# A decoder kernel whose statistics are summed by TensorE: two fp32r matmuls over a split operand for one plain fp32 matmul

## What is computed

```python
for l in range(DEPTH):                       # 2
    h = h + 0.5 * swiglu(rms(h, norm_ffn1), ffn1_wi, ffn1_wo)
    z = rms(h, norm_mix) @ w_in              # conv, spatial gate, q, k/v, gates
    y_a = conv_module(z_conv) @ conv_out     # depthwise conv of 31, LayerNorm over 512
    y_b = spatial_gating(z_sgu) @ sgu_out    # rms over 512
    y_c = nsa(q, k, v) @ nsa_out             # rms of every q and k head over 64
    h = h + (g_a * y_a + g_b * y_b + g_c * y_c) @ w_out
    h = h + cross_attention(rms(h, norm_xattn), rms(mem))   # k heads normed over 128
    h = h + 0.5 * swiglu(rms(h, norm_ffn2), ffn2_wi, ffn2_wo)
```

## Time and profile before

| | before |
|---|---|
| time, median of 3 runs | 2720.15 us (2715.23 to 2720.67) |
| span of the profiled execution | 2716.9 us |
| TensorE busy | 2664.1 us |
| VectorE busy | 1326.2 us |
| ScalarE busy | 1100.5 us |
| GpSimd busy | 1230.2 us |

### The profile page before, as it was taken

The page is one execution under the profiler, slowest core; times in us unless marked ns, Lnnn a source line. Parts: engine busy times, 40 slices in busy tenths (PEclk is TensorE's granted clock), DMA queues, the critical chain, the costliest instruction groups (busy, mean ns, idle before and its releaser), DMA issues.

```text
span 2716.9 us, 36975 instructions
## 1 busy us (share of the span) xinstructions
PE 2664.1 (98%) x13132; PEld 2137.3 (79%) x13132; DVE 1326.2 (49%) x1834; ACT 1100.5 (41%) x1664; POOL 1230.2 (45%) x616
## 2 busy tenths in 40 slices
PE   8999999989999999999999999999899999999999
PEld 6888888766678868888888888887667788788887
DVE  5221258786535554252541212777865364543533
ACT  5322242446644454222342223434476445542222
POOL 4444456672235424444444434567522354344443
PEclk9999999999999999999999999999999999999999
DMA  4334433222224313333333353432122342233332
GB/s 133 95 99 113 115 98 87 70 55 55 55 78 117 109 47 107 94 99 95 91 95 101 93 132 92 111 79 68 49 55 63 86 124 85 62 101 101 93 100 78
DMA packets 493612, 243.41 MB, mean 90 GB/s; under 512 B 49468, under 2 KB 491174, under 8 KB 493478
## 3 DMA queue, kind: packets, MB, share of 16 engines
q1 hardware_dynamic: 492960, 241.49, 32.0%
q10 hardware_dynamic: 518, 0.13, 0.0%
HBM read 239.46 MB, written 2.10 MB: 89 GB/s over the span
## 4 chain that ended last, share of the span: by engine, by line
PE 65%; issue 16%; POOL 8%; DVE 5%; ACT 3%; POOLq 2%; DVEq 1%; ACTq 0%; DMA 0%; SPq 0%
PE pg L636 20%; PE pg L639 19%; PE pg L642 19%; POOL wL L585 7%; PE pA L706 2%; DVE convb L1740 1%; PE pA L911 1%; PE pA L858 1%; POOLq L612 1%; POOLq L614 1%; DVE prob L1902 0%; POOL wsn L610 0%; ACT prob L1156 0%; ACT wH L1156 0%; ACT hH L1156 0%
## 5 line engine op out<-in xcount | busy, mean ns | idle before, releaser
L585 POOL TENSOR_TENSOR wL<-raw,wH 128x1024 fp32r<-128x1024 f32 (+1 forms) x472 | 1084.9, 2300 | 1453.2 <-ACT wH L1156 1449.4
L636 PE MATMUL pg<-gxH,wH 128*128 128x512 f32 (+1 forms) x2448 | 960.6, 392 | 3.6 <-DVE gxL L1601 3.1
L642 PE MATMUL pg<-gxH,wL 128*128 128x512 f32 (+1 forms) x2448 | 948.7, 388 | 0.0
L639 PE MATMUL pg<-gxL,wH 128*128 128x512 f32 (+1 forms) x2448 | 944.1, 386 | 0.0
L1156 ACT ACTIVATE wH<-raw 128x1024 fp32r<-128x1024 f32 (+1 forms) x472 | 475.8, 1009 | 834.3 <-PE pg L642 673.5
L636 PEld LDWEIGHTS pg<-gxH,wH 128*128 128x128 f32 x2448 | 461.0, 188 | 110.7 <-issue 18.4
L639 PEld LDWEIGHTS pg<-gxL,wH 128*128 128x128 f32 x2448 | 461.2, 188 | 93.6 <-issue 7.1
L642 PEld LDWEIGHTS pg<-gxH,wL 128*128 128x128 f32 x2448 | 461.0, 188 | 93.2 <-issue 3.9
L642 PE MATMUL pg<-hH,wL 128*128 128x512 f32 x992 | 392.7, 396 | 0.0
L636 PE MATMUL pg<-hH,wH 128*128 128x512 f32 x992 | 390.5, 394 | 1.5 <-DVE hL L1657 1.5
L639 PE MATMUL pg<-hL,wH 128*128 128x512 f32 x992 | 390.6, 394 | 0.0
(11 more groups left out here) (234 smaller groups left out, 2208.8 us busy)
## 6 DMA issues: line engine op xcount, KB each, us to landing
raw<-in_ffn_wi SPq DMA_DIRECT2D x352, 256.0 KB, 3.1
raw<-in_w_in SPq DMA_DIRECT2D x200, 256.0 KB, 3.3
raw<-in_ffn_wo SPq DMA_DIRECT2D x128, 256.0 KB, 3.0
raw<-in_ffn_wo SPq DMA_DIRECT2D x64, 192.0 KB, 2.6
raw<-in_xkv SPq DMA_DIRECT2D x32, 256.0 KB, 3.0
raw<-in_w_out SPq DMA_DIRECT2D x32, 256.0 KB, 3.0
raw<-in_sgu_out SPq DMA_DIRECT2D x32, 128.0 KB, 2.2
raw<-in_conv_out SPq DMA_DIRECT2D x32, 128.0 KB, 2.2
```

Source lines behind the costliest of these rows:

```text
L585: pool.tensor_tensor(wL[:, s % 4, 0:n, :], raw[:, s % 2, 0:n, :], wH[:, s % 4, 0:n, :].bitcast(F32), ALU.subtract)\
L636: mm(o, wH[:, s, k, :], rh(k), start=(k == 0), stop=False)
L639: mm(o, wH[:, s, k, :], rl(k), start=False, stop=False)
L642: last = mm(o, wL[:, s, k, :], rh(k), start=False, stop=(k == kt - 1))
```

## The change

Two fp32r tiles are added, `sacH` and `sacL`. Once `sacc` is complete, `stat_given` copies it to `sacH` (rounded to fp32r) and subtracts that from `sacc` into `sacL`, on VectorE, ahead of the semaphore. TensorE multiplies both, one after the other into the same bank. The ones matrices become fp32r tiles with fp32 views for the places that stay as they were, which are the 31-column statistic and the one-column matmuls.

```diff
         sacc = sb("sacc", [P, T])
+        sacH = sb("sacH", [P, T], F32R)
+        sacL = sb("sacL", [P, T], F32R)
...
-        ones = sb("ones", [P, P])
-        bdon = sb("bdon", [P, P])
+        onesR = sb("onesR", [P, P], F32R)
+        bdonR = sb("bdonR", [P, P], F32R)
+        ones, bdon = onesR[:, :].bitcast(F32), bdonR[:, :].bitcast(F32)
...
             def stat(l, s, weights, n=T):
 
                 pe.wait_ge(stat_in, risen(stat_in, l, s + 1 if s < 6 else s))
-                mm(pO[:, 0:n], weights[:, :], sacc[:, 0:n], start=True, stop=True)\
+                if n < T:
+                    mm(pO[:, 0:n], bdon[:, :], sacc[:, 0:n], start=True, stop=True)\
+                        .then_inc(stat_mm, 1)
+                    return
+                mm(pO[:, :], weights[:, :], sacH[:, :], start=True, stop=False)
+                mm(pO[:, :], weights[:, :], sacL[:, :], start=False, stop=True)\
                     .then_inc(stat_mm, 1)
...
                 def middle(key, s):
                     bank = t_bank(key)
                     pe.wait_ge(stat_in, risen(stat_in, l, s))
-                    weights = bdon if key in ("q2", "q3") else ones
-                    mm(bank[:, :], weights[:, :], sacc[:, :], start=True, stop=True)\
+                    weights = bdonR if key in ("q2", "q3") else onesR
+                    mm(bank[:, :], weights[:, :], sacH[:, :], start=True, stop=False)
+                    mm(bank[:, :], weights[:, :], sacL[:, :], start=False, stop=True)\
                         .then_inc(st_mm, 1)
...
             def stat_given(s):
 
+                dve.drain()
+                dve.tensor_copy(sacH[:, :], sacc[:, :])
+                dve.drain()
+                TTt(sacL[:, :], sacc[:, :], sacH[:, :].bitcast(F32), ALU.subtract)
                 dve.drain().then_inc(stat_in, 1)
...
                 def squares(src, n=T):
                     dve.drain()
                     TTt(sacc[:, 0:n], src, src, ALU.mult)
-                    stat_given(None)
+                    if n < T:
+                        dve.drain().then_inc(stat_in, 1)
+                    else:
+                        stat_given(None)
```

More of the change, by code:

```diff
@@ L678, in ffn @@
                                  before=norm_ready(l, n_norm) if c == 0 else None,
-                                 between=within(14, lambda: stat(l, s_norm, ones))
+                                 between=within(14, lambda: stat(l, s_norm, onesR))
                                  if c == 1 and s_norm else None)
                             if c == 1 and s_norm == 0:
-                                stat(l, s_norm, ones)
+                                stat(l, s_norm, onesR)
                         first = 1
@@ L738, in _ @@
                 unit(l, U_CONV + 1, 0, KD, gH, gL)
-                unit(l, U_CONV + 2, 0, KD, gH, gL, between=within(6, lambda: stat(l, 1, ones)))
+                unit(l, U_CONV + 2, 0, KD, gH, gL, between=within(6, lambda: stat(l, 1, onesR)))
                 for g in range(GROUPS):
@@ L747, in _ @@
                     unit(l, U_KV + j, 0, KD, gH, gL)
-                unit(l, U_KV + 4, 0, KD, gH, gL, between=within(6, lambda: stat(l, 2, bdon)))
+                unit(l, U_KV + 4, 0, KD, gH, gL, between=within(6, lambda: stat(l, 2, bdonR)))
                 v_rows(0)
                 unit(l, U_KV + 5, 0, KD, gH, gL)
-                stat(l, 3, bdon)
+                stat(l, 3, bdonR)
                 def cmp_ready(k):
@@ L795, in _ @@
                     if j == 2:
-                        stat(l, 5, bdon)
+                        stat(l, 5, bdonR)
                     if 3 <= j < 7:
@@ L802, in _ @@
                          lambda k: gxL[:, 4 * i + k, :])
-                stat(l, 7, bdon)
+                stat(l, 7, bdonR)
                 def gates_turned():
@@ L1017, in _ @@
                     if h == 4:
-                        stat(l, 12, ones)
+                        stat(l, 12, onesR)
                     if h == 6:
@@ L1027, in _ @@
                     if m == 0:
-                        stat(l, 13, ones)
+                        stat(l, 13, onesR)
                         xv_turned(1)
```

## The result

| | before | after |
|---|---|---|
| time, median | 2718.74 us (4 runs) | 2750.15 us (2748.06 to 2754.58, 4 runs) |
| ratio after / before | | 1.0116, 95% interval 1.0104 to 1.0128 |
| span of the profiled execution | 2716.9 us | 2746.3 us |
| TensorE busy | 2664.1 us | 2662.4 us |
| VectorE busy | 1326.2 us | 1378.4 us |

A forecast was written before the change was run, and what follows sets the result against it. TensorE, busy 98% of the span, was taken as the bound. Stalls of 16.75 us a layer, 33.5 for two, plus 0.5 in the prologue, less 10.9 saved, gave +23.1 us: 2743 us, range 2719 to 2757.

The forecast's parts named there:

- The bound and the sign: Whole kernel: TensorE, busy 98%, bounds it; stalls of 34.0 us less 10.9 saved make it 23.1 us slower.
- The saving per statistic: TensorE, 26 plain fp32 statistics become two fp32r matmuls: 0.42 us saved for each, 10.9 in all.
- The split, undisturbed: VectorE in stat_given: copy, subtraction and two drains raise the semaphore 1.28 us later when GpSimd doesn't interfere.
- The collisions by the timeline of before: Added copy and subtraction meet GpSimd's operations where they stand: 2.65 us at first key statistic, 2.6 at second, per layer.
- the FFN norm: Norm ahead of the second FFN: TensorE already waits, subtraction comes behind a wL; 3.4 us a layer, quiet 1.28.
- the norm before cross-attention: Added work unused there; a wL over the copy delays the query copy 3.4 us, TensorE 1.8; 1.2 taken a layer.
- s=7: Second query pair's statistic: a 2.40 us wL begins just ahead of the subtraction; stall 3.7 us, 3.0 taken a layer.
- Third query pair: Its squares: the split delays four convolution steps and the maxima TensorE waits for; 2.6 us a layer, quiet 1.28.
- the soaking rival: Attention stretch: existing TensorE waits and freer convolution steps absorb the added stalls; 7.1 us faster, 2713 us; chance 0.08.
- all others: Remaining statistics (mean, query pairs, memory keys, norms ending an FFN): slack of 2 us or more; 0.7 us a layer.
- The variance: Variance of the conv branch, GpSimd idle: 0.6 us a layer, up to 1.3 if a later transpose waits too.
- the prologue: First norm of the kernel: 0.5 us, between 0 and 1.1, added once.

The follow-up runs named there:

- the one-pass run: After without the split: the sum of squares written straight as fp32r, a single fp32r matmul for each statistic, low part left out; 2708.52 us, ratio 0.9954 to before.

## Why the prediction was right, and where it wasn't

- **The bound and the sign** were right: TensorE is the bound, its saving is 0.4% of the span, and the stalls outweigh it. That waits would take the place of matmul time in the order of 25 us was right to 1.3 us.
- **The saving per statistic** was 0.41, not 0.42. That all 26 would reach the end was wrong: 8.0 of 10.4 us did in the run without the split.
- **The split, undisturbed:** 1.28 forecast, 1.27 to 1.29 in every quiet one. The copy with fp32r output takes 0.43, as assumed from the fp32 copy.
- **The collisions by the timeline of before** were right almost to a tenth for four places: 2.65 against 2.52 at the first key, 2.6 against 2.51 at the second, 3.4 against 3.3 at the FFN norm, and 3.4 against 3.3 at the norm before cross-attention. At s=7 the timeline said 3.7 of stall and I took 3.0 for fear of a shift; it was 3.5, and 3.7 in the second layer. The discount was the error. At this place GpSimd, VectorE and TensorE had shifted by the same 5.6 us, so their relative position was kept.
- **The norm before cross-attention:** the working gave 1.8 for TensorE and took 1.2. The two waits there (for the drain, and for the squares of the queries behind it) cost 1.7 and 1.8 us in the two layers, so here too the discount was the error; the rest of the +3.4 in the first layer is the clock.
- **Third query pair:** this step failed. I took 2.6 a layer, 2.2 less the saving; it was -1.1 and -2.6. The split ran undisturbed, and of the four convolution steps behind it only one was held up by GpSimd (2.80 us, the others 0.75), where in before all four were (1.02 to 2.71):

```profile
594.72 0.43 DVE L1599 CAST sacH<-sacc 128x512 fp32r<-128x512 f32 x1
595.23 0.69 DVE L1601 TENSOR_TENSOR sacL<-sacc,sacH 128x512 fp32r<-128x512 f32 x1
596.03 5.28 DVE L1756 SCALAR_TENSOR_TENSOR convb<-convb,par 128x512 f32<-128x512 f32 x4
```

  Against 7.19 us for the four in the earlier trace rows they take 5.28 here, 1.9 less, which more than pays for the 1.27 of the split, and TensorE's wait for the maxima is 1.82 instead of 2.48. The engines' relative position was not kept here: the squares come 9.5 us later than in before, the `wL` of 128x1024 behind them only 7.3 (596.73 against 589.39). That was the mechanism of the soaking rival, and the freer port came true in this place. Of its other half, that TensorE's lateness is absorbed by waits that it had anyway, a part came true: ahead of the split, a wait of TensorE for ScalarE falls from 2.38 to 1.20 us in the first layer and one from 0.98 to nothing in the second. It is far from all, since after is still 8.7 us late at 620, counted from the first matmul.
- **The term that wasn't in the sum** is the clock. The forecast treated a wait as lost time alone. Behind five waits of 1.1 to 4.2 us the clock stood at half for 3.4 us. In the profiled pair, 29.4 us apart and so 6.3 over the forecast, the clock makes some 5 of these 6.3; between the medians, 8.3 over it, the estimate above makes it some 10. The terms at the norm before cross-attention (+3.4 in the first layer, where 1.2 was taken), at the FFN norm (+4.4 and +4.6 where 3.0 was) and at s=7 in the first layer (+4.9 where 2.6 was) hold it.
- **The last list, "all others",** 0.7 a layer, was too small: with the savings added back these places lost 3.7 us in the first layer and 2.0 in the second. The mean lost 1.3 and 1.0 by a wait behind its split, query pairs 0 and 3 some 0.4 each, the memory keys 1.5 in the first layer and 0.3 in the second. The variance, 0.6 a layer with 1.3 as its upper end, lost 1.6: by the wait for the drain (0.54) and by one at the next transpose (0.58 and 0.60), as the working had named them.
- **Luck in the total:** the third query pair was too high by some 8 us over both layers, and the cross-attention, taken at 0, came to -1.6 twice. Some 17 us of terms that were too low (s=7, the two norms, the variance, the others, the prologue) stand against these 11. The size is nearer than its parts.

What stays open: how much of the slowdown is waits and how much clock in the executions that weren't profiled; and how the 5 us missing in the one-pass run divide between the attention waits and the places of the half-clock stretches, which lie elsewhere in each kernel. It wasn't tried to have ScalarE make the copy, which would take one of the two collisions away.

## What to carry to other kernels

Before work is put ahead of a semaphore, look at who waits for that semaphore and how long ago it was raised when they came, and then at everything that is queued behind the work on its own engine. If VectorE and GpSimd both work in SBUF, price every two-input operation and copy of VectorE by what GpSimd runs at that moment, from the timeline; where all engines follow one bound engine that alignment can survive a shift of some microseconds (5.6 us at s=7, but not 9.5 at the third query pair), so take the price that it gives and don't discount it by feeling. Look also at the granted clock behind a new wait on TensorE. A few tenths saved on the bound engine count only as far as its next wait for another chain.

## What the runs showed of the hardware

- A VectorE copy of 128x512 from fp32 to fp32r takes 0.43 us undisturbed, as fast as fp32 to fp32, and up to 2.47 (878.93 in after) when a GpSimd subtraction is running.
- GpSimd's operations cost VectorE a good deal before this change already: with them cut, the kernel before is 33 us faster (ratio 0.9886, 0.9869 to 0.9902), though GpSimd is busy 45% only and TensorE waits 0.3 us for its `wL` in all.
- A plain fp32 matmul of 512 columns costs 0.88 us in the stream and an fp32r pair 0.47: 1.33 and 0.92 from neighbour to neighbour, less the 0.45 of two ordinary steps.
- Nine times in after TensorE waited over 1 us for the drain of a split. At five of these waits (1.05 to 4.17 us long) the clock fell to 1.2 GHz for 3.4 us, between 0.3 us before the wait ended and 2.1 us after; at four (1.19 to 3.67 us) it didn't: the length of the wait alone doesn't decide it. A matmul stream that lasts 3.4 us at half clock would have taken 1.7 at full clock, so such a wait costs 1.7 us more than it shows.
